# Output projection by column half instead of by token tile, in a block of attention, convolution, GLA and mixture of experts

## What is computed

```python
h = rms_norm(x, norm_mix)
# three branches (convolution, attention, GLA), gated and summed:
merged = sum(sigmoid(h @ w_merge_gate[n]) * (y_b @ w_branch[n]) for n, y_b in enumerate(branches))
x = x + merged @ w_out                      # the output projection
h2 = rms_norm(x, norm_ffn)
p_group = softmax(h2 @ w_rg + b_rg)         # router: 4 groups of 8 experts
le = (h2 @ w_re + b_re)                     # the two best experts of the best group
expert = (silu(xb @ w_g[e]) * (xb @ w_u[e])) @ w_d[e]      # 32 experts, width 512
x = x + weighted sum of each token's two experts
```

## Time and profile before

| what | value |
|---|---|
| median of 3 runs | 734.31 us (732.08 to 736.02) |
| profiled execution, its own time | 732.4 us |
| its span in the profile | 730.2 us |
| TensorE busy | 597.1 us, 82% |
| VectorE busy | 302.6 us, 41% |
| ScalarE busy | 194.4 us, 27% |
| read from HBM | 245.67 MB |
| chain that ended last | DMA 45%, PE 42%, DVE 7%, ACT 4% |

### The profile page before, as it was taken

How to read it: one execution, slowest core, us unless ns; L and a number is a source line. 1 busy time by engine, 2 the same in 40 slices (tenths; PEclk the granted TensorE clock), 3 DMA queues, 4 the chain that set the end, 5 groups by cost and what they waited for, 6 DMA issues and landing times.

```text
span 730.2 us, 15330 instructions
## 1 busy us (share of the span) xinstructions
PE 597.1 (82%) x6592; PEld 417.3 (57%) x6592; DVE 302.6 (41%) x620; ACT 194.4 (27%) x334; POOL 24.2 (3%) x55
## 2 busy tenths in 40 slices
PE   3999999999999898998656887578666877778775
PEld 3977789989999786654333443334333443334342
DVE  5457788865374756343231121311222121311232
ACT  4375446374344533311100110001100110001011
POOL 7002100000000000000000000000000000000000
PEclk9999999999999999999988687877977687778797
DMA  9973464543649639999999999999999999999994
GB/s 263 358 259 118 155 218 138 182 172 120 227 157 419 270 113 422 427 424 427 424 427 427 426 428 425 429 424 427 426 428 426 425 426 425 428 427 425 428 417 182
DMA packets 38531, 247.73 MB, mean 339 GB/s; under 512 B 4296, under 2 KB 4384, under 8 KB 24384
## 3 DMA queue, kind: packets, MB, share of 16 engines
q1 hardware_dynamic: 37008, 245.44, 83.1%
q0 software_dynamic: 912, 1.25, 0.8%
q10 hardware_dynamic: 544, 0.06, 0.1%
HBM read 245.67 MB, written 1.06 MB: 338 GB/s over the span
## 4 chain that ended last, share of the span: by engine, by line
DMA 45%; PE 42%; DVE 7%; ACT 4%; issue 2%; SPq 0%; DVEq 0%; ACTq 0%
DMA wide<-in_w_expert_up 39%; PE ps L1296 7%; PE ps L980 5%; PE ps L981 5%; PE ps L982 5%; DMA wide<-in_w_expert_down 4%; PE ps L1331 3%; DVE ring_lo L1416 3%; PE ps L1256 2%; PE ps L958 2%; PE ps L960 2%; PE ps L959 2%; DMA ring<-in_w_in 2%; ACT w_hi L683 2%; PE ps L1343 1%
## 5 line engine op out<-in xcount | busy, mean ns | idle before, releaser
L1296 PE MATMUL ps<-wide,xe 128*32 128x256 f32 x2048 | 166.4, 480 | 103.0 <-DMA wide<-in_w_expert_up 101.4
L1296 PEld LDWEIGHTS ps<-wide,xe 128*32 128x32 f32 x2048 | 78.4, 133 | 171.6 <-issue 132.0
L1764 DVE TENSOR_TENSOR xe<-ps,g_ffn 128x256 f32<-128x256 f32 x32 | 13.6, 424 | 259.1 <-PE ps L1265 259.1
L1416 DVE TENSOR_TENSOR ring_lo<-ring,w_hi 128x1024 fp32r<-128x1024 f32 x76 | 90.7, 1222 | 45.4 <-ACT w_hi L683 43.2
L980 PE MATMUL ps<-hT_hi,w_hi 128*128 128x256 f32 x320 | 90.7, 283 | 3.6 <-DVE ring_lo L1416 3.6
L981 PE MATMUL ps<-hT_lo,w_hi 128*128 128x256 f32 x320 | 89.5, 280 | 0.0
L982 PE MATMUL ps<-hT_hi,ring_lo 128*128 128x256 f32 x320 | 89.4, 280 | 0.0
L683 ACT ACTIVATE w_hi<-ring 128x1024 fp32r<-128x1024 f32 x76 | 78.4, 1056 | 40.2 <-PE ps L982 28.5
L980 PEld LDWEIGHTS ps<-hT_hi,w_hi 128*128 128x128 f32 x320 | 61.1, 191 | 4.9 <-issue 4.7
L1331 PE MATMUL ps<-wide,he 128*32 128x256 f32 x1024 | 62.5, 382 | 1.0 <-DMA wide<-in_w_expert_down 1.0
L886 ACT ACTIVATE he<-ps 128x128 f32<-128x128 f32 x32 | 8.9, 277 | 201.4 <-PE ps L1311 198.8
(11 more groups left out here) (272 smaller groups left out, 775.3 us busy)
## 6 DMA issues: line engine op xcount, KB each, us to landing
wide<-in_w_expert_gate SPq DMA_DIRECT2D x27, 2048.0 KB, 45.2
wide<-in_w_expert_up SPq DMA_DIRECT2D x27, 2048.0 KB, 48.3
wide<-in_w_expert_down SPq DMA_DIRECT2D x27, 2048.0 KB, 40.4
ring<-in_w_in SPq DMA_DIRECT2D x9, 2048.0 KB, 13.7
ring<-in_w_merge_gate SPq DMA_DIRECT2D x6, 2048.0 KB, 10.1
wide<-in_w_expert_gate SPq DMA_DIRECT2D x10, 1024.0 KB, 10.8
wide<-in_w_expert_up SPq DMA_DIRECT2D x10, 1024.0 KB, 11.0
wide<-in_w_expert_down SPq DMA_DIRECT2D x9, 1024.0 KB, 12.4
```

The costliest lines, as they stand in the source:

```text
L1296: ins = t_.matmul(ps[q * WIN:(q + 1) * WIN, b, 0:QW], xe[b][:, k % 2, k // 2, :], w, start=(k == 0), stop=(k == KD - 1))
L1416: v.tensor_tensor(ring_lo[g % PRE_RING][:, chunk(c)], ring[g % PRE_RING][:, chunk(c)], out_hi[g == 19][c][:, :].bitcast(F32), ALU.subtract ...
```

## The change

In all three places that name a projection by number, `2 * tt + half` becomes `2 * half + tt`: the projections are counted in the order (0, 0), (1, 0), (0, 1), (1, 1), written (tile, half). TensorE makes them in this order. The transposes of tile 0, which stood inside the third projection, now stand inside the first part of the fourth and wait for the third addition. The first transposes of tile 1 follow that part, and only then comes the router product of tile 0. Units 12 to 15 wait for the second projection instead of the third. On VectorE the addition of (1, 0) and the square sum of its 512 columns come second, the addition of (1, 1)'s first part comes ahead of `pick(0)`. On ScalarE `x1_high(0)` moves from between the copies of the two tiles to behind `x1_root(1)`.

```diff
--- before.py
+++ after.py
@@ -522,7 +522,7 @@
                 elif n == 10:
                     sp.wait_ge(branch_done, 12)
                 elif n < 16:
-                    sp.wait_ge(proj_done, first_bank[NPRE - 2] + 3)
+                    sp.wait_ge(proj_done, first_bank[NPRE - 2] + 2)
                 elif n != 20:
                     sp.wait_ge(proj_done, first_bank[NPRE])
                 else:
@@ -836,11 +836,11 @@
             x1_root(0)
             x1T_out(0, 0, 4, 1)
             x1T_out(0, 4, 8, 1)
-            x1_high(0)
             x1T_out(1, 0, 4, 2)
             x1T_out(1, 4, 6, 3)
             x1T_out(1, 6, 8, 4)
             x1_root(1)
+            x1_high(0)
             act.wait_ge(proj_done, first_bank[NPRE])
             x1_high(1)
 
@@ -1152,7 +1152,7 @@
 
             def out_proj(tt, half, ks=range(KD), part=None):
 
-                r = first_bank[18] + 2 * tt + half
+                r = first_bank[18] + 2 * half + tt
                 b = r % 4 if part != 1 else 3
                 if ks[0] == 0:
                     if part == 1:
@@ -1198,16 +1198,15 @@
                     ins.then_inc(router_mm, 1)
 
             out_proj(0, 0)
+            out_proj(1, 0)
             out_proj(0, 1)
-            out_proj(1, 0, range(0, 4))
-            turn_x1(0, range(KD), 2)
-            out_proj(1, 0, range(4, KD))
+            out_proj(1, 1, range(0, 4), 0)
+            turn_x1(0, range(KD), 3)
+            out_proj(1, 1, range(4, KD), 0)
+            turn_x1(1, range(0, 4), 3)
             pe.wait_ge(router_ready, 1)
             route(0, range(0, 4), 1)
             route(0, range(4, KD), 2)
-            out_proj(1, 1, range(0, 4), 0)
-            turn_x1(1, range(0, 4), 3)
-            out_proj(1, 1, range(4, KD), 0)
             out_proj(1, 1, range(0, 5), 1)
             route(1, range(0, 4), 3)
             turn_x1(1, range(4, 6), 4)
@@ -1684,7 +1683,7 @@
                 at = half * C + (n if part == 1 else 0)
                 xv = x_tok[:, tt, at:at + n]
                 v.tensor_tensor(xv, xv, bank(r % 4 if part != 1 else 3)[:, 0:n], ALU.add).then_inc(x1_ready, 1)
-                dve.wait_ge(x1_ready, 2 * tt + half + 1 + (part == 1))
+                dve.wait_ge(x1_ready, 2 * half + tt + 1 + (part == 1))
 
             def square_sum(tt, cols, at):
 
@@ -1715,14 +1714,14 @@
                 v.tensor_tensor(below[:, tt, :, :], every, chosen, ALU.is_gt).then_inc(assign_ready, 1)
 
             x1_add(0, 0)
+            x1_add(1, 0)
+            square_sum(1, slice(0, C), 33)
             x1_add(0, 1)
             square_sum(0, slice(0, D), 32)
             v.tensor_scalar(stat[:, 36:37], stat[:, 32:33], 1.0 / D, EPS, ALU.mult, ALU.add).then_inc(ms2_ready, 1)
             scale_out(0)
-            x1_add(1, 0)
+            x1_add(1, 1, 0)
             pick(0)
-            square_sum(1, slice(0, C), 33)
-            x1_add(1, 1, 0)
             square_sum(1, slice(C, C + C // 2), 34)
             link(v.tensor_scalar(stat[:, 35:36], stat[:, 33:34], stat[:, 34:35], None, ALU.add))
             x1_add(1, 1, 1)
```

## The result

| | before | after |
|---|---|---|
| median of 20 runs each | 733.94 us (731.0 to 737.41) | 735.87 us (733.07 to 738.74) |
| profiled execution, its own time | 732.4 us | 735.14 us |
| its span in the profile | 730.2 us | 732.9 us |

After to before is 1.0032, with a 95% interval of 1.0020 to 1.0045: 0.3% slower, some 2.3 us. The interval leaves out zero, but the size is within the 0.5% that counts as no difference here. The forecast was 736.6 us in a range of 732.8 to 739.6, with +2.9 us for the change.

The account below looks back on a forecast made before the run. The prediction took the expert-weight stream's start and later rests to bound the kernel; ScalarE's 1.5 us plus the clock's 1.4 us gave +2.9 us, set against a mean of 733.7: 736.6 us, range 732.8 to 739.6.

Parts of the forecast that it names:

- The early transfers: Units 12 to 15 issued 6.4 us earlier, units 16 to 19 unmoved at 279.39; nearly all of the gain lost again.
- The rest of the DMA engines: Engines idle from 275.8 to 281.26 us, between units 12 to 15 and units 16 to 19.
- The cap of 0.4 us on the gain: With pair 22/23 still issued at 294.64, the stream would go on at 296.5 instead of 296.9.
- ScalarE: Moved tile 0 scaling shifts `tab`, `xe` and pair 22/23 by 1.85 us; stream loses 1.5 us.
- The clock: TensorE waits 2.7 us before the first gate/up half, falls to 1.2 GHz; taken as 1.4 us.
- the two modes: Clock fall: first half alone slow, 1.4 us; or row selection and second half slow too, 3.2 us.
- The sum: 1.5 us and 1.4 us give +2.9 us on the profiled execution; set against a mean of 733.7: 736.6 us.
- rival (2): TensorE's clock holds through the wait before the first half: +1.5 us, 735.2 us; chance 0.17.
- rival (4): Early transfers of units 12 to 15 count in full: -6.4 us, 727.3 us; chance 0.05.
- rival (3): Moved ScalarE scaling is short, 0.8 us net, TensorE waits 1.6 us: +0.4 us, 734.1 us; chance 0.04.
- rival (1): TensorE's clock stays low longer, row selection after the first half at half speed: +4.7 us, 738.4 us; chance 0.25.
- TensorE and VectorE in the new order: Reordered projections, transposes and picks cost nothing, slack 0.5 us at tile 0's transposes; under 0.5 us if one slack fails.

Follow-up runs that it names:

- after with the step in the gap: The changed kernel with the scaling of tile 0 (L828) put behind the copy of tile 1's first four blocks; ratio 1.0006 to the kernel before.
- the second trace of after: The changed kernel run again unchanged, beside later kernels; ratio 1.0039 to the kernel before.
- the new order: As a run: the changed kernel with last projection finished before the remaining router work, tile 0 scaled behind its root, both picks last, `xe` early; 0.9959 to the kernel before.

## Why the prediction was right, point by point

**The early transfers: right.** 12 to 15 were to leave 6.4 us earlier with 16 to 19 in their place, and that is what the queue shows (15.38 us apart, 8.93 before). The rest of the DMA engines was forecast for 275.8 to 281.26, 5.5 us; it stands at about 274.9 to 280.3, 5.4 us, and some 0.9 us earlier, in a trace in which 16 to 19 leave 0.77 us earlier. (From 274 to 277 us the stream moves 352, 25 and 16 GB/s, that is 0.92 us' worth at 427; from 279 to 282 it moves 123, 205 and 410, 1.73 us' worth.) The cap of 0.4 us on the gain couldn't be resolved: after with the step in the gap, where the cap would show, measured between -0.8 and +1.6 us.

**ScalarE: right, and 0.2 us too dear.** 1.85 us were taken for the net shift, 1.64 to 1.65 measured in six traces. The two scalings take 4.17 us together, less than the 2.15 + 2.29 of the single rows. Reading L828 by its own rows was what counted. L828 reads every eighth fp32 value, 32 bytes apart, and took 2.15 us where the contiguous L683 took 1.04; 512 columns with the same stride took 1.22 us. The Trainium skill, "SBUF — State Buffer", section "Door 1: The DMA port swizzle", says that an access that crosses to a new line of 16 bytes pays a penalty; by that rule the slowness is the stride's, and the trace agrees (2.15 against 1.04 us). L683 and L828 also differ in the output type and in L828's scale operand, and no run here changed the stride alone, so the cause is argued, not shown.

**The clock: right that it falls, the price too low.** Forecast was a wait of 2.7 us, measured 2.69. The first of the two modes was priced at 1.4 us and the second at 3.2, with nothing between. Measured, from the first half's start to the issue of 22/23 against before's 4.54: +1.69 us in three kernels and in the second trace of after, +2.67 in its first. The term was mis-sized because in the rows of the later stage I let the first half pay alone. There another product, 1 us long, stands between the half and the row selection; here the row selection follows at once, and it paid too: 1.21 to 1.96 us for 1.07. The two modes were not clean in before either: in two of the six short cases that I counted, the row selection took 1.46 us (at 342.66) and 1.36 us (at 701.25).

```profile
342.66 1.46 PE L1256 MATMUL ps<-xn,pick_w 128*32 128x256 f32 x16
```

Taking the fall away, by nine matmuls whose result goes nowhere, took most of the loss away (1.0005, or 1.0 us by the medians).

**The sum.** 1.5 + 1.4 = 2.9 us; with the measured terms it would be 1.3 + 1.7 = 3.0 us. The two errors nearly cancel, and that is luck. With the long fall of the first trace it would be 3.9, more than either comparison measured; how often which fall comes, two traces can't tell. The measured change, by ratio, is 2.3 and 2.9 us. The time alone would not have decided between the forecast and rival (2): 735.87 us is 0.7 from 736.6 and 0.7 from 735.2. Rival (2), the clock holds, is refuted by the granted clock of 0.50; rival (4), the full gain, by the first hole; rival (3), a short ScalarE step, by 4.17 us for two. Of rival (1) the profiled execution shows the very sign that was to decide against the forecast, a row selection at nearly half speed (1.96 us), with a second half of 2.10 us; its price of 2.67 us is nearer to that rival's 3.2 than to my 1.4. The rival's time, 738.4, did not come, and the second trace has the shorter fall.

**TensorE and VectorE in the new order: right.** The third addition at 268.86 ends at 269.55, and the transposes start at 270.00 without a wait. With the step in the gap the rest of the change costs nothing that can be measured.

**What was not seen.** That the price of the moved step hangs on the order around it. In the new order the same step costs nothing that was measured, since other engines are last. The prediction says "nothing hides it there", which is true of both kernels it compared, and no more than that.

## What to carry to other kernels

When a stream is fed by a ring, count from issue to issue: an early issue is worth only as much as the next gated issue lets it, and each later one costs from the point at which its cover of a few tenths of a microsecond is used up. A step moved off an idle spot is to be priced twice, by what it adds to the chain, and by what the longer wait does to TensorE's clock right behind it; here the second (1.7 or 2.7 us) was larger than the first (1.3). To gain from releasing memory early, move the last release too: the new order, in which the next four units are issued 3.3 us earlier, gained 3 us.

## What was unexpected of the hardware

- One fp32 matmul of 128x128 with `ident` counts as two records and takes 0.23 to 0.24 us (twenty of them: 40 records in 4.63 us; nine: 18 records in 2.17 us). Whoever counts records to size such a filler gets twice the time.
- TensorE kept 2.4 GHz over waits of 1.19, 1.46 and 1.52 us and was at 1.2 GHz after waits of 2.17, 2.69, 2.70 and 2.75 us in the same place. When it falls and how long it stays low differs between executions of one program: in the first trace of after it fell within the wait already (PEclk 0.77 from 289 to 290 us, 0.50 from 290 to 296, 0.82 from 296 to 297), in the second only after the first half had started (1.00 from 291 to 292, 0.56 from 292 to 293, 0.50 from 293 to 295, 0.74 from 295 to 296). That is the difference between the two prices. The second half was back at full speed in all but one trace.
- The stream comes back from a rest somewhat sooner than I took from units 12 to 15 (1.87 us after the issue). In after, 22/23 are issued at 298.11, and of the three microseconds from 299 to 302, at a mean of 333 GB/s, 2.34 us' worth at 427 GB/s was moved: as if from 299.66 on, 1.55 us after the issue.

```profile
296.00:299.00 3.00, 2.89 (x43) 1.85 (x36) 0.35 (x1) 2.43 (x3) 0.00 (x0) 0.94 0.00 0
299.00:302.00 3.00, 3.00 (x45) 2.14 (x43) 1.26 (x5) 2.00 (x4) 0.00 (x0) 1.00 1.00 333
```
